# A hybrid encoder layer on one core: the first twenty microseconds in a new order

## The reference

```python
h = rmsnorm(x, norm_mix_w[l])      # x * rsqrt(mean(x*x) + eps) * w
proj = h @ w_in[l]                 # 1024 x 1024 by 1024 x 3600
gq, gk, gv, ggate, ga, dq, dk, dv, dgate = split_cols(proj)
g_logit = (ga @ w_alpha2[l] + b_alpha2[l]).astype(f32)
g = jax.nn.log_sigmoid(g_logit) / GLA_TAU
```

## Time and profile before

| | |
|---|---|
| median of 3 runs | 825.1 us (824.53 to 827.13) |
| the profiled execution | 825.03 us |
| its span, first to last instruction | 823.3 us |
| PE busy | 809.1 us, 98% of the span |
| DVE busy | 574.7 us, 70% |
| ACT busy | 430.6 us, 52% |
| POOL busy | 85.7 us, 10% |

### The profile page before, as it was taken

One profiled execution on the slowest core, in us unless ns is written; L12 is line 12 of the kernel. 1 busy time (PEld: TensorE's weight loads), 2 busy tenths in 40 slices (PEclk: granted clock), 3 DMA queues, 4 the chain that ended last, 5 costly groups with the idle time before them and its releaser, 6 DMA issues.

```text
span 823.3 us, 12950 instructions
## 1 busy us (share of the span) xinstructions
PE 809.1 (98%) x4472; PEld 678.9 (82%) x4472; DVE 574.7 (70%) x1330; ACT 430.6 (52%) x1041; POOL 85.7 (10%) x122
## 2 busy tenths in 40 slices
PE   8999999999999999999999999999999999999996
PEld 7878888887788888888888898888888888888885
DVE  6688566665678668767757877599836454367997
ACT  6775445443455445445546576644645454366443
POOL 3100122211010111111000001010110000001201
PEclk9999999999999999999999999999999999999999
DMA  8321369952223255545512178954422111206945
GB/s 292 115 83 39 91 192 205 193 121 65 87 88 109 84 99 109 114 84 122 108 63 74 58 227 248 295 124 124 150 81 77 39 64 52 78 13 143 216 91 204
DMA packets 70408, 99.19 MB, mean 120 GB/s; under 512 B 6596, under 2 KB 38472, under 8 KB 70344
## 3 DMA queue, kind: packets, MB, share of 16 engines
q1 hardware_dynamic: 52360, 64.29, 24.5%
q0 software_dynamic: 15392, 29.36, 19.6%
q10 hardware_dynamic: 2592, 4.72, 1.7%
HBM read 83.68 MB, written 31.46 MB: 140 GB/s over the span
## 4 chain that ended last, share of the span: by engine, by line
PE 90%; DVE 7%; ACT 2%; issue 1%; DMA 0%; POOL 0%; ACTq 0%; DVEq 0%
PE bank L1860 14%; PE bank L1862 14%; PE bank L1861 14%; PE banks2to L1860 10%; PE banks2to L1862 10%; PE banks2to L1861 10%; PE banks6to L1932 4%; PE banks2to L2126 3%; PE bank L2149 2%; DVE neg_max L1659 2%; DVE w_lo L1395 1%; PE banks2to L2066 1%; PE bank L2151 1%; DVE prT_lo L1394 1%; DVE actT_lo L1394 1%
## 5 line engine op out<-in xcount | busy, mean ns | idle before, releaser
L1862 PE MATMUL bank<-w_hi,actT_lo 128*128 128x512 f32 x412 | 161.4, 392 | 0.0
L1860 PE MATMUL bank<-w_hi,actT_hi 128*128 128x512 f32 x384 | 154.9, 403 | 0.7 <-DVE gate L1549 0.4
L1861 PE MATMUL bank<-w_lo,actT_hi 128*128 128x512 f32 x384 | 149.6, 390 | 0.0
L1395 DVE SCALAR_TENSOR_TENSOR w_lo<-w_raw,vecs,w_hi 128x512 fp32r<-128x512 f32 x120 | 86.8, 749 | 27.2 <-ACT w_hi L1111 27.2
L1862 PEld LDWEIGHTS bank<-w_hi,actT_lo 128*128 128x128 f32 x412 | 77.3, 188 | 17.1
L1111 ACT ACTIVATE w_hi<-w_raw,vecs 128x512 fp32r<-128x512 f32 x120 | 82.5, 720 | 7.1 <-DMA w_raw<-in_w_ckv 3.8
L1860 PEld LDWEIGHTS bank<-w_hi,actT_hi 128*128 128x128 f32 x384 | 72.1, 188 | 16.2 <-DVE w_lo L1395 1.5
L1861 PEld LDWEIGHTS bank<-w_lo,actT_hi 128*128 128x128 f32 x384 | 72.3, 188 | 12.9
L997 POOL TENSOR_TENSOR rs_o<-var_o,neg_half 128x1 f32<-128x1 f32 (+1 forms) x48 | 31.1, 647 | 369.1 <-DVE var_o L1686 256.8
L1862 PE MATMUL banks2to<-w_hi,actT_lo 128*128 128x512 f32 x164 | 64.0, 390 | 0.0
L1278 ACT ACTIVATE prob<-banks2to,neg_maxs 128x128 f32<-128x128 f32 (+7 forms) x64 | 46.9, 740 | 15.1 <-DVE neg_maxs L1660 15.0
(11 more groups left out here) (373 smaller groups left out, 2009.7 us busy)
## 6 DMA issues: line engine op xcount, KB each, us to landing
w_raw<-in_w_in SPq DMA_DIRECT2D x56, 256.0 KB, 3.8
out_sums<-in_w_out POOLq DMA_DIRECT2D x11, 1024.0 KB, 10.0
late_sums<-in_w_co POOLq DMA_DIRECT2D x11, 1024.0 KB, 9.0
w_raw<-in_w_ckv SPq DMA_DIRECT2D x32, 256.0 KB, 3.4
w_raw<-in_w_cq SPq DMA_DIRECT2D x32, 256.0 KB, 2.7
stage_in<-in_x SPq DMA_DIRECT2D x8, 512.0 KB, 4.6
tile_a<-mixed ACTq DMA_DIRECT2D x16, 256.0 KB, 3.4
x_res<-in_x SPq DMA_DIRECT2D x8, 512.0 KB, 6.8
```

The source lines that it names most:

```text
L1395: return dve.scalar_tensor_tensor(dst, src, scale, hi.bitcast(F32), ALU.mult, ALU.subtract)
L1860: pe.matmul(dst, l_hi, r_hi, start=start, stop=False)
L1861: pe.matmul(dst, l_hi, r_lo, start=False, stop=False)
L1862: return pe.matmul(dst, l_lo, r_hi, start=False, stop=stop)
```

## The change

The beginning of the list is written anew, and the norm's weights for the mixing get a transfer, a semaphore (`d_mix`) and a turning of their own.

- ACT issues the transfer of the mixing norm's weights as its first instruction; SP issues the other six small ones, behind tile 2.
- SP's order becomes: tiles 0 and 1, weight 0, tile 2, the six small transfers, weight 1, tile 3, and the rest as before.
- Stage `vec` turns and copies the eight mixing columns alone; it stands behind the first 18 fillers and ahead of the first scaling. The other columns and the positions are stage `vec2`, in bank 0, behind the fourth tile's turning, the cast of the positions and weight 2. `gate`, the rotary angles and the turning of the fifth tile wait for the second copy.
- Weight 0 is split between the scalings of tiles 0 and 1; tile 2 is scaled and turned ahead of the first product; tile 3 is squared behind the turning of tile 2, scaled between the two half products (`G0h`) and turned behind them.
- The fillers, 24, 2, 6 and 10 before, are 18, 8, 4, 2, 4 and 6; the last six stand behind `vec2`, in bank 1.

```diff
-    plan = [("zeros",), *normed(0), *normed(1), ("sq", 2), *busy(0, 24), ("tr", 0, 0), ("pos",), ("scale", 2), ("tr", 0, 1)]
-    plan += [*busy(1, 2), ("tr", 1, 0), ("vec",), ("tr", 1, 1), *busy(2, 6), ("sq", 3), ("w", 0), ("tr", 2, 0), ("scale", 3)]
-    plan += [("tr", 2, 1), *busy(3, 10), ("G0h", 0), ("w", 1), *tr(3), ("G0h", 1), ("w", 2), ("const",)]
+    plan = [("zeros",), ("sq", 0), *busy(0, 18), ("vec",), *busy(1, 8), ("scale", 0), ("sq", 1), ("w", 0), ("scale", 1)]
+    plan += [("sq", 2), *tr(0), ("scale", 2), *busy(2, 4), *tr(1), ("w", 1), *busy(3, 2), *tr(2), ("sq", 3), *busy(4, 4)]
+    plan += [("G0h", 0), ("scale", 3), ("G0h", 1), *tr(3), ("pos",), ("w", 2), ("vec2",), *busy(5, 6), ("const",)]
...
-            for t in range(3):
-                load_input(t)
+            load_input(0)
+            load_input(1)
+            load_weight(0)
+            load_input(2)
             for dst, src in (
-                (vec_rows[0:8, :], a["norm_mix_w"][0].rearrange("(k p) -> k p", p=P)),
...
-            load_weight(0)
+            load_weight(1)
             load_input(3)
-            load_weight(1)
...
+            act.dma_start(vec_rows[0:8, :], a["norm_mix_w"][0].rearrange("(k p) -> k p", p=P)).then_inc(d_mix, 16)
...
                 elif kind == "vec":
                     dve.wait_ge(vec_pe, 1)
-                    then_wait(dve.tensor_copy(vecs[:, :], banks[5][:, 0:28]))
-                    dve.tensor_copy(pos_f[:, :], banks[5][:, 28:36]).then_inc(vec_dve, 1)
+                    dve.tensor_copy(vecs[:, 0:8], banks[5][:, 0:8]).then_inc(vec_dve, 1)
+                elif kind == "vec2":
+                    dve.wait_ge(vec_pe, 2)
+                    dve.tensor_copy(vecs[:, 8:28], banks[0][:, 8:28])
+                    dve.tensor_copy(pos_f[:, :], banks[0][:, 28:36]).then_inc(vec_dve, 1)
...
+                    if w[0] == 5:
+                        pe.wait_ge(tr_dve, at("tr", 2, 1))
                     for _ in range(w[1]):
-                        pe.transpose(banks[7][:, 0:P], ident[:, :], ident[:, :])
+                        pe.transpose(banks[1 if w[0] == 5 else 7][:, 0:P], ident[:, :], ident[:, :])
                 elif kind == "vec":
                     pe.wait_ge(pool_c, 4)
-                    pe.wait_ge(d_vec, 16 * 7)
+                    pe.wait_ge(d_mix, 16)
+                    pe.transpose(banks[5][:, 0:8], vec_rows[0:8, :], ident[0:8, 0:8]).then_inc(vec_pe, 1)
+                elif kind == "vec2":
+                    pe.wait_ge(d_vec, 16 * 6)
                     pe.wait_ge(pos_dve, 1)
-                    pe.transpose(banks[5][:, 0:28], vec_rows[:, :], ident[0:28, 0:28])
-                    pe.transpose(banks[5][:, 28:36], pos_rows[:, :], ident[0:TT, 0:TT]).then_inc(vec_pe, 1)
+                    pe.wait_ge(tr_dve, at("tr", 2, 1))
+                    pe.transpose(banks[0][:, 0:28], vec_rows[:, :], ident[0:28, 0:28])
+                    pe.transpose(banks[0][:, 28:36], pos_rows[:, :], ident[0:TT, 0:TT]).then_inc(vec_pe, 1)
...
+                    if t == 4:
+                        pe.wait_ge(vec_dve, 2)
```

## The result

The changed kernel takes 828.15 us (median of 11 runs, 827.12 to 830.31), the kernel before beside it on the same chip 825.23 (11 runs, 824.53 to 827.13). The ratio is 1.0037, with a 95% interval from 1.0029 to 1.0045: about 3.0 us slower, where 1.7 were forecast. The time lies in the forecast range, but it is slower by more than 0.3%, to which the prediction gave 21%. Three single executions among those of the experiments took 1140 to 2835 us; the ratios leave them out, and as one of them is the only profiled one of e12_shift16_at_585, that kernel has times alone.

The account below looks back on a forecast made before the run. TensorE (PE), busy 98% of the span, was taken as the bound; the fourth tile's 0.9 and the vectors' 0.8 to 0.9 move `ga` from 18.5 to 20.2, +1.7 on 825.1: 826.8 us, range 824.4 to 828.6.

Parts of the forecast that it names:

- The chain: Start up to `ga`: summed handoffs put the first product near 13.4, 0.8 early, and `ga` at 20.2 instead of 18.5.
- The two terms: Ahead of `ga`: the fourth tile's later square loses 0.9, the late vectors behind it another 0.8 to 0.9.
- rival 3: Start: the mixing weights land late, near 8.0, delaying ACT's weight and third square by 1.1: 827.9; 6%.
- rival 4: Fourth tile's scaling: POOL's gate weight work holds DVE off in full, costing 0.8: 827.5; 6%.
- less than the lock: DVE scaling beside POOL's cast: grew by 0.11, ending at 15.48, not near 15.7 as the skill's exclusive port lock implies.
- rival 2: Behind PE's stand from 17.6 to 19.5: TensorE falls to its lower level, 2.7 us on top: 829.5; 8%.
- its signs: Fillers or gate products behind the hole ahead of `ga` at 0.216 apiece would show the forecast wrong.
- whatever shifts the moment from which it does so shifts the end by as much: PE from `ga` on runs nearly without holes, so a shift of `ga` reaches the end unchanged: +1.7 us.
- the forecast's own 1.7: At `ga`: the forecast shift of PE's work, 20.2 - 18.5 = +1.7 us, carried to the end.
- Rival 1: From first product to `ga`: the early product's 0.8 is carried through, 824.3, or 825 if only part stays; 17%.

Follow-up runs that it names:

- e12_shift16_at_585: The kernel before with sixteen fillers on PE ahead of a turning at about 585 us: 827.03 us, ratio 1.0021.
- e11_before_shift16: The kernel before with sixteen fillers between the second half product and `ga`: 827.73 us, ratio 1.0032.
- e5_both: The changed kernel with the fourth tile's square, scaling and turning earlier, `vec2` behind `ga`, and fillers moved: 825.13 us, ratio 1.0001 to the kernel before.
- e4_sq3_early: The changed kernel with the fourth tile's square, scaling and turning earlier, `vec2` still ahead of `ga`: 825.67 us, ratio 1.0015 to the kernel before.
- e9_no_last_fillers: The changed kernel without the six fillers behind `vec2`: 827.66 us, ratio 1.0032 to the kernel before.
- e3_before_hole: The kernel before without the ten fillers ahead of the first product: 824.91 us, ratio 1.0000.

## Why the prediction was right and wrong

**The chain was right.** ACT's third square came at 8.30 (forecast 8.1), the first high part at 9.36 (9.36), the first product at 13.26 (13.4), the fourth square at 13.63 (13.62), the fourth scaling at 15.69 (15.76), the fourth turning at 16.63 (16.68), the cast at 19.16 (19.14), the vectors' turning at 19.47 (19.49). That the first high part agrees to the hundredth is luck: the third square was 0.2 late, but ACT began the high part 1.06 behind it and not 1.26. The 1.26 is the distance of two squares; from the square at 11.57 to the weight behind it at 12.61 it was 1.04 already. The two terms are shown by themselves: with the vectors out of the way `gate` keeps 1.04, with the fourth tile early it keeps nothing. The mixing weights were in time: their copy stands at 6.08, the scaling behind it at 6.69, so rival 3 fell. So did rival 4:

```profile
15.62 0.41 POOL L1005 TENSOR_TENSOR ga_raw<-ga_raw,vecs 128x128 f32<-128x128 f32 x1
16.09 0.85 POOL L1010 CAST ga_both<-ga_raw 128x384 fp32r<-128x384 f32 x1
```

DVE's scaling at 15.69 began inside the first of these POOL operations, ran into the second, and took 0.89, against 0.75 alone and 0.86 counted. The first operation took 0.41, not the 0.87 of the earlier trace rows from which the rival's price was reckoned, so even a full wait would have been 0.34 here. By the Trainium skill's page SBUF — State Buffer ("Who interferes with whom") the scaling would have had to wait until 16.03 and then hold the second operation off; it ended at 16.58, 0.2 sooner than that. But the second operation took 0.85, against 0.51 in the earlier trace rows, so one did hold the other off, and as POOL's spans are rough, 0.2 does not settle it: the prediction's "less than the lock" is not shown.

**From `ga` on it was wrong, in two steps.** The first is rival 2, "TensorE falls to its lower level", to which I gave 8%, "against: the level was the upper one behind 0.70 of idle". It came, in the profiled execution and, by mean clocks of 0.997 or less, in up to six of the ten others, four of them clear at 0.996 or less. The forecast named its signs (fillers or gate products at half pace behind the hole). Its price was 1.7 and not 2.7, since it lasted 3.4 and not 5.4: 0.5 to 0.7 in the six fillers and the turnings ahead of them, and 1.0 in the products of `ga` (from `ga` to `gate` 29.15 - 20.90 = 8.25, against 25.77 - 18.50 = 7.27). One short hole that had kept the level was no evidence for a hole of 1.74.

The second is the sentence that "whatever shifts the moment from which it does so shifts the end by as much". The sixteen fillers of e11_before_shift16 are the forecast's own 1.7 with nothing else of the change: they cost 2.6 and not 1.7 or 1.8, by the ratio 1.0032. That is where the executions of the changed kernel that kept a mean clock of 0.999 lie as well (827.12 to 827.55, against 827.18 to 828.42 there). I had read PE's waits and found no line over 0.7 behind 45 us; I did not look at which weights of PE were only just in time.

**What adds up to the median and what does not.** In the profiled execution the sum closes without the second step: 1.7 of the chain and 1.7 of the level are the 3.4 at `gate` and at the end. In the executions at 0.999 it would close without the first, with 1.7 of the chain and some 0.9 of the stretch behind 476 us; none of them was profiled. The median ratio of the change (1.0037) and that of the bare shift (1.0032) overlap, so what the level adds to the median is not settled; filling the hole, which keeps the level up and takes out 0.8 of the shift with it, gave back 1.4.

Rival 1 fell: the first product is 1.0 earlier and the half products are done ahead of the fourth tile's turning, but `ga` needs all four tiles. e5_both shows that even an earlier `ga` gave nothing at the end.

## What to carry to other kernels

A product that is made earlier is worth nothing if the last of its companions is made later: in this start the fourth tile sets the end, and moving its square of 1.06 behind two high parts, with the scaling and turning that follow it, cost more than all that the new order gained. Look at the wait ahead of a long dense stretch as a hole as well, and put fillers into it and not behind it: behind it six of them were a cost, 0.63 at the upper level (17.82 to 18.45 in e4_sq3_early) and 1.19 at the lower. And don't take a shift of the bounding engine's work as carried one to one through a stretch in which its operands land just in time; count those landings too, and give the shift a price with a spread.

## What the runs showed of the hardware

Behind the same hole of 1.74 at the same place, with another of 1.50 or 1.66 some 7.5 us ahead, TensorE fell to its lower level for 3.4 us in one profiled execution and stayed at the upper one in another (e9_no_last_fillers), and behind one of 1.69 five microseconds earlier, in the kernel before, it stayed (e3_before_hole). The granted clock rose again at about 22.9, while `ga`'s products ran. The spread of the kernel before, 824.46 to 825.92 us in all but three of the 94 executions beside the experiments, is of the size of what the stretch of 476 to 525 us adds or doesn't (-0.1 to 1.35 in the table); that the one comes from the other is not shown. In e11_before_shift16 a weight was used there 1.2 us later against its request (2.99 - 1.82).
